# Expert sum kept feature-major into the next layer, the norm's factor moved behind the first products, and buffers placed by address

## What is computed

```python
# end of the first block
x = x + peer(rms_norm(x, norm2_g), w_query, sub_keys, expert_u, expert_v)   # 16384 experts
x = rms_norm(x, final_norm_g)              # x * r * g, r = 1/sqrt(mean(x*x) + eps) for each token
# each of the two layers of the second block
proj = x @ w_in                            # 1024 -> 4680 columns
qA, kA, vA, gA, qB, kB, vB, gB, qI, kI, wI = split(proj)
oA = stick_breaking_attention(qA, kA, vA)
oB = dsa_sparse_attention(qB, kB, vB, qI, kI, wI, rel_bias, topk=64)
y = concat([oA * silu(gA), oB * silu(gB)]) @ w_out
x = layer_norm(ALPHA * x + y, ln_g, ln_b)
```

## Time and profile before

| | |
|---|---|
| median of 3 runs | 1360.52 us (1360.25 to 1362.12) |
| the profiled execution | 1360.35 us, of which the span of instructions is 1358.6 us |
| busy share of PE, PEld, DVE, ACT, POOL | 95%, 91%, 53%, 50%, 49% |
| mean granted clock of TensorE | 0.981 of 2.4 GHz |
| expert sum | 623 to 983 us |
| from its end to the layer's first product | 983.0 to 997.6 us |
| layer 0, layer 1 | 997.6 to 1166, 1178 to the end |

### The profile page before, as it was taken

The page is one execution under the profiler, slowest core; times in us unless marked ns, Lnnn a source line. Parts: engine busy times, 40 slices in busy tenths (PEclk is TensorE's granted clock), DMA queues, the critical chain, the costliest instruction groups (busy, mean ns, idle before and its releaser), DMA issues.

```text
span 1358.6 us, 26713 instructions
## 1 busy us (share of the span) xinstructions
PE 1295.7 (95%) x9912; PEld 1237.1 (91%) x9912; DVE 719.2 (53%) x1474; ACT 678.7 (50%) x1208; POOL 671.3 (49%) x287
## 2 busy tenths in 40 slices
PE   7988999999999999999999999999979999799996
PEld 5877999899999999999999999999979987699875
DVE  2444059992056666675555555555525632446423
ACT  5555444344555555554444444444434654346552
POOL 6736769999856666663000000000056665567653
PEclk9989999999999999999999999999989999899998
DMA  6724435445534444445555555555554343434432
GB/s 222 259 78 165 165 137 177 172 164 181 184 135 139 141 141 142 140 140 193 187 186 190 189 189 186 185 185 187 169 201 148 132 140 112 152 135 146 141 123 78
DMA packets 59108, 218.57 MB, mean 161 GB/s; under 512 B 6632, under 2 KB 6664, under 8 KB 58656
## 3 DMA queue, kind: packets, MB, share of 16 engines
q1 hardware_dynamic: 56592, 206.07, 44.8%
q0 software_dynamic: 1760, 8.95, 1.8%
q10 hardware_dynamic: 688, 2.62, 0.5%
HBM read 215.50 MB, written 4.21 MB: 162 GB/s over the span
## 4 chain that ended last, share of the span: by engine, by line
PE 82%; issue 6%; POOL 6%; DVE 3%; ACT 1%; DMA 1%; POOLq 0%; DVEq 0%; ACTq 0%
PE A L489 27%; PE W L489 18%; POOL ringl L444 5%; PE A L513 5%; PE A L514 4%; PE A L518 4%; PE W L750 4%; PE A L532 4%; PE A L534 4%; PE A L539 4%; PE W L566 1%; PE W L891 1%; POOL ringl L409 1%; PE W L625 1%; PE W L862 1%
## 5 line engine op out<-in xcount | busy, mean ns | idle before, releaser
L409 POOL TENSOR_TENSOR ringl<-ring,ringh 128x1024 fp32r<-128x1024 f32 x139 | 341.4, 2468 | 193.6 <-ACT ringh L939 186.4
L444 POOL TENSOR_TENSOR ringl<-ring,ringh 128x1024 fp32r<-128x1024 f32 x126 | 320.1, 2546 | 114.9 <-ACT ringh L1099 83.7
L489 PE MATMUL W<-XTh,ringh 128*128 128x256 f32 x1024 | 296.7, 290 | 6.6 <-POOL ringl L444 6.5
L489 PE MATMUL W<-XTl,ringh 128*128 128x256 f32 x1024 | 290.7, 284 | 0.0
L489 PE MATMUL W<-XTh,ringl 128*128 128x256 f32 x1024 | 290.4, 284 | 0.0
L489 PE MATMUL A<-Hh,ringh 128*128 128x256 f32 x1024 | 285.8, 279 | 0.5 <-DVE Hl L1479 0.5
L489 PE MATMUL A<-Hl,ringh 128*128 128x256 f32 x1024 | 285.8, 279 | 0.0
L489 PE MATMUL A<-Hh,ringl 128*128 128x256 f32 x1024 | 285.7, 279 | 0.0
L939 ACT ACTIVATE ringh<-ring 128x1024 fp32r<-128x1024 f32 x135 | 141.9, 1057 | 153.7 <-PE A L518 67.6
L489 PEld LDWEIGHTS W<-XTh,ringh 128*128 128x128 f32 x1024 | 194.8, 190 | 8.0 <-issue 7.7
L1099 ACT ACTIVATE ringh<-ring 128x1024 fp32r<-128x1024 f32 x189 | 197.3, 1044 | 1.5 <-PE A L489 1.5
(11 more groups left out here) (247 smaller groups left out, 2102.6 us busy)
## 6 DMA issues: line engine op xcount, KB each, us to landing
ring<-exp_u SPq DMA_DIRECT2D x128, 512.0 KB, 3.2
ring<-exp_v SPq DMA_DIRECT2D x128, 512.0 KB, 3.5
ring<-w SPq DMA_DIRECT2D x72, 512.0 KB, 3.2
ring<-w_out SPq DMA_DIRECT2D x24, 512.0 KB, 3.2
ring<-w_in SPq DMA_DIRECT2D x20, 512.0 KB, 3.4
ring<-w_query SPq DMA_DIRECT2D x16, 512.0 KB, 3.2
skewed<-scratch POOLq DMA_DIRECT2D x1, 2048.0 KB, 11.3
H<-lng POOLq DMA_DIRECT2D x2, 1024.0 KB, 5.7
```

The lines of the kernel that those rows point to most:

```text
L409: pool.tensor_tensor(ringl[:, slot, :], ring[:, slot, :], ringh[:, slot, :].bitcast(F32), ALU.subtract)\
L444: pool.tensor_tensor(ringl[:, slot, :], ring[:, slot, :], ringh[:, slot, :].bitcast(F32), ALU.subtract)\
L489: last = pe.matmul(dst, stationary[a], moving[b], start=start and n == 0, stop=stop and n == 2, skip_group_check=True)
```

## The change

The end of the expert sum no longer goes through token-major form before the layer starts:

- Early on, POOL issues one more DMA (the final norm's g as 8 rows, `GF`); at the start of the expert sum PE transposes it into a column for each chunk, and ACT keeps it (`gain[:, 3, :]`).
- Inside the expert sum, behind its unit 122, PE transposes the kept x (16 transposes), and in the four turns after it ACT copies the result to `XTF`.
- After the sum DVE adds y to `XTF` chunk by chunk (8 additions, `v_done`), ACT and DVE make XTh and XTl of it with g as the scale. Chunks 4 to 7 go first, and the first group's units are loaded and used in that order, because this group writes the banks that hold chunks 4 to 7 of y.
- PE transposes x+y to token-major behind the group's part 0, for the sum of squares on ACT and for X. Behind part 2 it spreads r over the partitions in two matmuls, and ACT keeps this as `RB`.
- In layer 0 the results of q and k groups are multiplied by RB, on DVE; those of v and g groups get r as ACT's scale. kI and the indexer's weights are scaled on DVE.
- DVE makes the low parts of the layer's units 0 and 1 within the last turns of the expert sum; POOL made them after it.
- `home` pads the addresses: XTh at 128 and the ring at 256 past a multiple of 512, as before, and Hh at 192, where it was 288.

```diff
+TURN_AT = 6 * DOWN_TURNS + 2
+FIRST_CHUNKS = [4, 5, 6, 7, 0, 1, 2, 3]
...
+        def home(first):
+            n = (first - nc.sbuf_base) % 512
+            if n:
+                sb(f"gap{nc.sbuf_base}", [P, n // 4])
...
+        home(192)
         Hh = sb("Hh", [P, 2, T], F32R)
...
-            for u in range(U_LAYER, U_LAYER + SLOTS):
-                split_low(u)
-            pool.wait_ge(y_added, NB)
+            split_low(U_LAYER + SLOTS - 1)
             pool.wait_ge(skew_out, 16)
...
+            pe.wait_ge(end_gain, 16)
+            pe.transpose(W4[:, 0, 0:KC], GF[:], ident[0:KC, 0:KC]).then_inc(end_turned, 1)
             down(U_DOWN % SLOTS, 0, first=True)
...
-            pe.wait_ge(y_out, 2)
-            for tb in range(NB):
-                for m in range(KC):
-                    last = pe.transpose(W4[:, 2 * tb + m // 4, (m % 4) * P:(m % 4 + 1) * P], YT[:, m, tb * P:(tb + 1) * P],
-                                        ident)
-            last.then_inc(y_back, 1)
+                if n == TURN_AT:
+
+                    pe.wait_ge(x_in, 32)
+                    for c in range(KC):
+                        for tb in range(NB):
+                            last = pe.transpose(W8[:, c, tb * P:(tb + 1) * P], X[:, tb, c * P:(c + 1) * P], ident)
+                    last.then_inc(xt_done, 1)
...
-                else:
-                    transpose_pass(X, rows_ready, 4 * NB)
...
+                            if layer == 0 and j < 2:
+                                pe.wait_ge(v_done, 4 * (j + 1))
+                            if layer == 0 and LAYER_GROUPS[j] == "kI":
+                                pe.wait_ge(rb_ready, 1)
...
+                        elif layer == 0 and j == 0:
+                            unit_cols(b0, FIRST_CHUNKS[2 * part] // 2, part == 0, part == 3)
+                            if part == 0:
+
+                                pe.wait_ge(v_done, KC)
+                                for tb in range(NB):
+                                    for c in range(KC):
+                                        last = pe.transpose(W4[:, 2 * tb + c // 4, (c % 4) * P:(c % 4 + 1) * P],
+                                                            XTF[:, c, tb * P:(tb + 1) * P], ident)
+                                    last.then_inc(v_back, 1)
+                            if part == 2:
+
+                                pe.wait_ge(r_ready, NB)
+                                for tb in range(NB):
+                                    last = pe.matmul(A4[:, 0, tb * P:(tb + 1) * P],
+                                                     stat[:, tb, 3:4].broadcast_to([P, P]), ident, start=True, stop=True)
+                                last.then_inc(rb_done, 1)
...
-                if n == NK - 1:
-                    act.activation(YT[:, 0:4, :], A8[:, 0:4, :], ACT.Copy).then_inc(y_out, 1)
+                if TURN_AT < n <= TURN_AT + 4:
+                    b = n - TURN_AT - 1
+                    act.wait_ge(xt_done, 1)
+                    act.wait_ge(hl_done, KC)
+                    act.activation(XTF[:, 2 * b:2 * b + 2, :], W8[:, 2 * b:2 * b + 2, :], ACT.Copy).then_inc(xt_kept, 1)
...
             step(act.activation(primer[:, 0:1], zeros[:, 0:1], ACT.Sqrt))
-            for tb in range(NB):
-                act.wait_ge(y_added, tb + 1)
-                rms(tb, X[:, tb, :], MIX[:, tb, :], D, 0)
-            split_high(U_LAYER + SLOTS)
+            act.wait_ge(end_kept, 1)
+            for at, c in enumerate(FIRST_CHUNKS):
+                act.wait_ge(v_done, at + 1)
+                act.activation(XTh[:, c, :], XTF[:, c, :], ACT.Copy, scale=gain[:, 3, c:c + 1]).then_inc(tr_act, 1)
+                if at == 3:
+                    split_high(U_LAYER + SLOTS)
+            for tb in range(NB):
+                act.wait_ge(v_back, tb + 1)
+                rms(tb, W4[:, 2 * tb:2 * tb + 2, :].rearrange("p a b -> p (a b)"), MIX[:, tb, :], D, 0)
...
+                        if layer == 0 and arg[0] == 2:
+                            act.wait_ge(rb_done, 1)
+                            act.activation(RB[:, :], A4[:, 0, 0:T], ACT.Copy).then_inc(rb_ready, 1)
...
-                if u < U_LAYER:
+                if u < U_LAYER + SLOTS - 1:
                     next_low(u + 1, u % SLOTS)
             dve.wait_ge(unit_used, U_LAYER)
...
+            def first_low(chunks):
+                for at, c in enumerate(chunks):
+                    dve.wait_ge(tr_act, high_seen[0] + at + 1)
+                    ins = dve.scalar_tensor_tensor(out=XTl[:, c, :], in0=XTF[:, c, :], scalar=gain[:, 3, c:c + 1],
+                                                   in1=XTh[:, c, :].bitcast(F32), op0=ALU.mult, op1=ALU.subtract)
+                    if c % 2:
+                        ins.then_inc(tr_lo, 1)
+                high_seen[0] += len(chunks)
+
+            dve.wait_ge(xt_kept, 4)
+            for part in (FIRST_CHUNKS[:4], FIRST_CHUNKS[4:]):
+                for c in part:
+                    dve.tensor_tensor(XTF[:, c, :], A8[:, c, :], XTF[:, c, :], ALU.add).then_inc(v_done, 1)
+                first_low(part)
...
+                    elif step_name == "out" and layer == 0 and LAYER_GROUPS[arg][0] in "qk":
+                        g = g0 + arg
+                        dve.wait_ge(unit_used, units_through(g))
+                        dve.wait_ge(rb_ready, 1)
+                        for b in range(2):
+                            c = slice(4 * (g % 2) + 2 * b, 4 * (g % 2) + 2 * b + 2)
+                            dve.tensor_tensor(features[LAYER_GROUPS[arg]][:, 2 * b:2 * b + 2, :], A8[:, c, :],
+                                              RB[:, :].unsqueeze(1).broadcast_to([P, 2, T]), ALU.mult)\
+                                .then_inc(grp_free[g % 2], 1)
```

More of the change, by code:

```diff
@@ L197, in program @@
         X = sb("X", [P, NB, D])
+        home(128)
         XTh = sb("XTh", [P, KC, T], F32R)
         XTl = sb("XTl", [P, KC, T], F32R)
-        gain = sb("gain", [P, 3, KC])
+        gain = sb("gain", [P, 4, KC])
+        RB = sb("RB", [P, T])
+        GF = sb("GF", [KC, P])
         bias_s = sb("bias_s", [P, NH])
         w_idx2 = sb("w_idx2", [P, LAYERS * KC, 2, NH], F32R)
+        home(256)
         ring = sb("ring", [P, SLOTS, UNIT])
@@ L318, in program @@
         col_done = sem("col_done")
-        h_final, y_out, y_back, y_added = (sem(n) for n in ("h_final", "y_out", "y_back", "y_added"))
+        h_final, xt_done, xt_kept, v_done, v_back, end_gain = (sem(n) for n in (
+            "h_final", "xt_done", "xt_kept", "v_done", "v_back", "end_gain"))
+        r_ready, rb_done, rb_ready, x_back = sem("r_ready"), sem("rb_done"), sem("rb_ready"), sem("x_back")
+        end_turned, end_kept = sem("end_turned"), sem("end_kept")
         rel_done, rel_out = sem("rel_done"), sem("rel_out")
@@ L380, in _ @@
             for layer in range(LAYERS):
-                load(w2[layer, 0, 0]), load(w2[layer, 0, 1]), load(w2[layer, 0, 2]), load(w2[layer, 0, 3])
+                for j in range(4):
+                    load(w2[layer, 0, j if layer else FIRST_CHUNKS[2 * j] // 2])
                 load(w2_ki[layer])
@@ L421, in _ @@
                     pool.dma_start(keysT.rearrange("p a k -> p (a k)"), skT).then_inc(wst_in, 16)
+                    pool.dma_start(GF[:], bass.AP(rows.tensor, D, [[P, KC], [1, P]])).then_inc(end_gain, 16)
                 if u == 3 * SLOTS:
@@ L520, in unit_rows, with unit_cols @@
                 used(last)
-            def unit_cols(b0, j):
+            def unit_cols(b0, j, first=None, final=None):
+                first, final = j == 0 if first is None else first, j == 3 if final is None else final
                 u = unit[0]
@@ L531, in unit_cols @@
                     k, f = 2 * j + kk, slice(m * P, (m + 1) * P)
-                    pe.matmul(A8[:, 2 * b0 + m, :], wh[:, kk, f], XTh[:, k, :], start=k == 0 and m % 2 == 0, stop=False,
+                    pe.matmul(A8[:, 2 * b0 + m, :], wh[:, kk, f], XTh[:, k, :], start=first and kk == 0 and m % 2 == 0, stop=False,
                               skip_group_check=True)
@@ L1128, in _ @@
             act.dma_start(X[:], x_kept.rearrange("(b p) d -> p b d", p=P)).then_inc(x_in, 16)
+            act.wait_ge(end_turned, 1)
+            act.activation(gain[:, 3, :], W4[:, 0, 0:KC], ACT.Copy).then_inc(end_kept, 1)
             with act.Fori(0, DOWN_TURNS) as i:
@@ L1167, in _ @@
                         act.wait_ge(unit_used, units_through(g))
-                        if name == "kI":
+                        if layer == 0 and name[0] in "qk":
+                            pass
+                        elif name == "kI":
                             act.activation(KIT, A4[:, 2 * (g % 2), 0:T], ACT.Copy).then_inc(grp_free[g % 2], 1)
@@ L1516, in _ @@
+            dve.wait_ge(x_back, NB)
             for layer in range(LAYERS):
                 g0 = G_LAYER + G_PER_LAYER * layer
-                transposed_low(4 + 2 * layer, None)
+                if layer:
```

(11 more changed lines are left out.)

28 lines of the change are left out of this document (14 added, 14 removed).

## The result

The changed kernel takes 1344.13 us (median of 4 runs, 1342.75 to 1345.12) where the kernel before takes 1360.38 in the same comparison: a ratio of 0.9879, interval 0.9862 to 0.9896. That is 16.2 us less. I forecast 8.6 less, with a range that ended at 1350.8: the sign was right and the size was not.

What follows compares the result with a forecast made beforehand. PE, busy nearly everywhere, bounds the kernel; the target was its hole between expert sum and layer. From 1360.35, +2.09 (transposes in the sum) - 12.89 (gap) + 2.22 (group's new PE work) = -8.6 us, to 1351.8; range 1350.8 to 1356.5.

Steps and rivals of the forecast that it cites:

- step 1: Inside the expert sum: 16 transposes of x (+1.97 us) and one of g (0.12), copies on ACT covered; +2.09 us.
- rival C: Expert sum: Hh's address sets PE's matmul pace; if 192 is like 128, +11.4 us, to 1363.2; total chance 0.13.
- the good side: Expert sum at Hh's new address runs faster, pace 0.1067, saving up to 31 us; chance of beating the range 0.03.
- the bad side: Expert sum at Hh's new address runs slower, 3.7 ns more per matmul, +11.4 us, to 1363.2; chance 0.06.
- Steps 2 to 4: Gap behind the expert sum: first product 2.4 us after its end, part 0 done at 5.25 instead of 18.14; -12.89 us.
- Step 5: Layer's first group: 16 transposes behind part 0 (1.97 us) and two matmuls for RB (0.25); +2.22 us.
- Step 6: Layer's start: XTl's low parts wait for POOL, r and kI's low part follow; all hidden, thinnest cover 0.7 us.
- Rival A: Behind part 0: POOL also holds DVE's additions, PE waits 1.7 us, time 1353.5; chance 0.07.
- Steps 7 and 8: Layer 0's q and k results on DVE (cover 2.2 us) and POOL's DMA for GF: cost 0 each (DMA 0.5 if not).
- rival B: Layer 0: DVE's queue becomes the wait, giving back 2 to 5 us, to 1354 to 1357; chance 0.07.
- The clock: Gap of 2.4 us idle PE: clock taken to hold, two in three; a fall would cost 1.7 us.

Runs made afterwards that it cites:

- the last with transpositions: The changed kernel with XTh 256, ring 320, Hh 256, plus a small transposition ahead of every sixth unit of the expert sum: 1344.36 us (1341.03 to 1344.45).
- TensorE alone: Kernel's work left out, PE alone runs streams of 96 matmuls at varied operand bases: for 256 columns, 10.91 us a stream at moving base 192, 11.50 at 0.

## Why the prediction missed, step by step

**The step that failed** is step 1 together with rival C: "the sum's pace stays 0.1168". I had seen that the base might set the pace, wrote of the good side "nothing speaks for that" and gave it 0.03, and gave the bad side 0.06. What I had were two points, 0.1168 at 288 and 0.1205 at 128, and the question whether 192 is like 128. Runs show that it is like neither: the distance from the stationary operand counts, modulo 256, and 64 below it is the one fast value among those tried, 0.1134. It gave 10.2 us, more than all the rest of the change. Rival C's mechanism was real on both sides, but that its bad case of 1363.2 stands so near the 1363.6 measured is luck: it was reckoned from the pace at 128 for a base of 192, and came at 256.

**The gap** was read rightly. Steps 2 to 4: the additions began at E + 0.03 (0.1 forecast) and took 0.33 each from start to start (0.34 forecast), first product at E + 2.5 (2.4), part 0 at full clock in the profile shown. The table load did not wait for E. With the old pace the change gives 7.7 us, against 8.6.

**Step 1** otherwise: the sum with its additions runs from 625.50 to 975.85, 350.35; its matmuls are 348.4 of it, so the added transposes, 1.75 and 0.20 in the chain, cost 1.95, 2.09 forecast. Of the 1.1 us by which it starts later I had nothing in the sum, and the scatter between profiles of one kernel is as large. **Step 5**: the two instructions for RB stand as four matmuls in the trace, 0.49 us and not 0.25. The transposes behind part 0 waited for nothing. **Step 6**: the low parts waited for POOL's end as forecast (2.91), the additions didn't; kI had no wait. Rival A is refuted by the row at 978.80. What I had read from the rows of DVE beside POOL came true in both halves: the four low parts with two operands in SBUF waited (2.91 us, and 1.66 without POOL), the four additions with one in PSUM did not (1.42 both times). **Steps 7 and 8**: no new wait of PE in the layer; rival B did not come.

**The clock.** I took two in three that it holds in a gap of 2.4 us. Of seven profiles with a gap of 2.5 it held in three: in the changed kernel, in that with Hh at 256 and in the last with transpositions. In the other four it fell within about 1.4 us of part 0's start and stayed low for some 3.3; the windows of the changed kernel with Hh at 288, whose part 0 starts at 988.28:

```profile
988.50:989.50 1.00, 1.00 (x10) 1.00 (x10) 1.00 (x4) 0.83 (x2) 0.41 (x1) 1.00 0.81 246
989.50:990.50 1.00, 1.00 (x8) 1.00 (x6) 1.00 (x3) 1.00 (x4) 1.00 (x1) 0.58 1.07 209
990.50:991.50 1.00, 1.00 (x6) 1.00 (x6) 1.00 (x1) 0.39 (x1) 1.00 (x2) 0.50 0.72 270
```

3.3 us at half clock cost 1.7, as forecast; only the weight was off. What I missed is that the fall behind kI also varies from profile to profile, with kernels that differ in nothing there: some 6.5 to 7 us of it in all three profiles whose clock held in the gap, and some 3.3 in three of the four whose clock fell there (6.8 in the fourth, with XTh at 192). So in six of seven the low stretches behind the sum add up to about 6.5 to 7 us, and a held clock in the gap saved nothing.

**What stays open.** The pace is not fixed by the distance to the last per cent: the stretch of the upward product with XTh at 128 took 60.74 us in the kernel before and 60.07 in the changed kernel with the same bases, and a base of 288 gave 0.1167 in the kernels and 0.1178 with TensorE alone. The slow pace at the fast distance was never seen with TensorE alone, in a few streams only. Why 64 below the stationary operand is fast, what in the first matmuls of a stretch selects a pace, and why the stretches of 144 alternate. The runs show that these are so, not why.

## What to carry to other kernels

Before arguing about what surrounds a long stream of matmuls, read its pace from the chain (time over count) and compare it between streams of one shape; when a change moves a buffer, put each buffer's base beside it, and treat the pace as a term of the sum that the change can touch. One more buffer moved from 128 to 192 gave 16 us here, twice what the rewrite of the gap gave, and TensorE alone over all bases shows in one run which distances are worth trying. And when executions fall in two groups, profile until both have been seen: the rows named the place at once, and three theories about waits were wrong.

## What the runs showed of the hardware

- A float32r stream of 256 columns ran at 0.1134 to 0.1212 us per matmul by the distance of the moving operand's base from the stationary one's, modulo 256 bytes; 0.1134 only at 64 below, and 4 bytes to either side of it 0.120.
- For 512 columns the two operands at the same base were best, 21.77 us for 96 matmuls, then the moving one 64 above, 21.99; all other distances took 22.3 to 22.5.
- At the fast distance the same stream has a second pace, 0.1179, which it can keep for 350 us; the upward product, with XTh at the same distance, ran at 0.1133 in one kernel and at 0.1178 in another. With Hh at 192 and a transposition of 8 x 128 just ahead of it 17 of 17 executions were fast, and 16 of 32 without; with all bases moved by 64, two of four in spite of it.
- The granted clock after one and the same idle time of 2.5 us fell in four profiles and held in three.
